# First row norm of a three-layer block: warm-up by products of zeros, rows turned by products with scaled identities, sinks written by ScalarE

## The chip, the cores and the metric

The kernel runs on one core of a Trainium2 chip. The metric is device time in microseconds (us), the median of several executions. A profiled execution gives the trace; its span runs from the first to the last instruction of the program, and the execution's own time lies a little above it.

## What is computed

The input x has 512 rows of 1024 channels, float32. A hybrid block (pooling branch and mLSTM branch) and two attention layers follow one another. Cut to what the change touches:

```python
def rms_norm(x, g):
    xf = x.astype(jnp.float32)
    y = xf * lax.rsqrt(jnp.mean(xf * xf, axis=-1, keepdims=True) + EPS)
    return (y * g.astype(jnp.float32)).astype(x.dtype)

h = rms_norm(x, norm_pre_g)              # [1, 512, 1024], the first norm
proj = jnp.einsum('bsd,de->bse', h, w_in)  # everything else of the block starts here
...
# even attention layer: 6 query heads with a window of 128 keys and one sink logit per head:
# the sink stands beside the keys in the softmax and has no value row
```

## The kernel before

**The stages.** The product of two float32 matrices is made of three products of reduced operands: each operand is split in a head (`hi`) and a rest (`lo`), both of the type float32r. ScalarE writes the heads of the weights and VectorE the rests (for a few units GpSimd writes both), and TensorE accumulates three products of 512 columns each (lines 1763 to 1765). The stages (gates, u, za, mix, ga, pa, qk, v, and so on up to the two attention layers) follow each other in an order that is written out by hand, one queue per engine; there is no planner. Weights come in units of 1 MB into three slots, loaded from SyncE's queue.

**The first norm.** The 512 rows are 4 tiles of 128 rows (`TT = 4`), the 1024 channels 8 tiles (`KT = 8`). TensorE needs the normalised rows with channels on the partitions, so each of the 32 blocks of 128x128 has to be turned. Four tiles of x are loaded on SyncE's queue, the identity on ScalarE's. ScalarE squares the tiles 0, 1 and 3 with a sum along each row (`square`, line 785) and takes the root (`root`, line 790); VectorE squares tile 2 itself (line 1234) and ScalarE takes its root at line 831. VectorE makes the reciprocal (line 1209) and scales the 1024 columns of the tile into `xnrow` (line 1210). TensorE first turns the identity 8 times for warm-up (`WARM`, line 1879), then turns the 8 blocks of each tile as it comes (line 1884), into eight banks, one per channel tile. Only the last row tile completes the banks and signals `tr_ready`. Then ScalarE writes the head of each of the 8 channel tiles with the gain (line 797), VectorE the rest (line 1216), and TensorE starts the first stage (gates), 24 products that each wait for their channel tile, and then the stage u, whose first weights VectorE splits behind the 8 rests (line 1185).

**The sinks.** In the even layer the probabilities of a pair of heads stand in `pr`, with the sink in the column behind the keys. For 12 pairs VectorE copies the sinks there (line 1652) just ahead of the two instructions that add the bias to the logits and find the least (line 1654). ScalarE takes the exponential over keys and sink (line 1134), and VectorE the reciprocal of its sum (line 1629). TensorE turns the probabilities (line 2162), VectorE copies them (line 1669), and TensorE multiplies them with the values (line 2174); between these TensorE computes the gate z of the same layer with products of the usual kind. GpSimd splits z's weights at the same time (lines 694 and 695).

Of the kernel before, what the change touches and what calls it, by code (L numbers as in the profile page):

```python
# [10 lines left out]
ACT = mybir.ActivationFunctionType  # L11
ALU = mybir.AluOpType
AX = mybir.AxisListType

P = 128
D = 1024
KT = D // P
S = 512
TT = S // P
# [1 line left out]
SLOT = KT * UC  # L21
SLOTS = 3
EPS = 1e-6
WARM = 8
BIG = 1e30
FLOOR = -3e38

# [19 lines left out]
A_HEADS, B_HEADS, C_HEADS, M_HEADS = 6, 6, 12, 4  # L47
# [7 lines left out]
VC = {}  # L55
# [65 lines left out]
def hybrid_block_then_two_attention_layers(nc, A, vecs_d, consts_d, out):  # L121
    stack = ExitStack()
    with stack:
        base = (nc.sbuf_base + 63) // 64 * 64
        K = 1024

        def at(name, shape, offset, dt=F32):
            return nc.alloc_sbuf_tensor_at(name, shape, dt, offset=base + offset)

        def sem(name):  # L130
            return stack.enter_context(nc.semaphore(name))


        HT, OP, RAW, WHI, R0, R1, R2, R3, R4, CST = (
            0, 32 * K, 64 * K, 88 * K, 112 * K, 128 * K, 144 * K, 160 * K, 177 * K, 193 * K)
# [11 lines left out]
        ident = at("ident", [P, P], CST)  # L147
        bones = at("bones", [P, P], CST + 512)
        vecs = at("vecs", [P, NVEC], CST + K)
# [12 lines left out]
        small = at("small", [P, 24], CST + 14 * K + 768)  # L162

        xrow = at("xrow", [P, TT, D], R4)
        xnrow = at("xnrow", [P, TT, D], R0)
        rowmax_all = at("rowmax_all", [P, 2, S], CST + 7 * K)
        zaT = at("zaT", [P, KT, S], R0)
        uT = at("uT", [P, KT, UW], R1)
# [36 lines left out]
        pr = at("pr", [P, 6, S], R0 + 4 * K)  # L205
# [20 lines left out]
        ident_in = sem("ident_in")  # L226
# [3 lines left out]
        x_in = [sem(f"x_in{t}") for t in range(TT)]  # L230
# [13 lines left out]
        eps_ready = sem("eps_ready")  # L244
        rsd_ready = sem("rsd_ready")
        xn_ready = sem("xn_ready")
        xsq_by_vector = sem("xsq_by_vector")
        tr_ready = sem("tr_ready")
        tr_hi = sem("tr_hi")
        tr_lo = sem("tr_lo")  # L250
# [45 lines left out]
        hn_done = sem("hn_done")  # L296
# [4 lines left out]
        prT_ready = sem("prT_ready")  # L301
# [3 lines left out]
        o_ready = sem("o_ready")  # L305
        x_rows = sem("x_rows")
        logit_ready = sem("logit_ready")
        part_hi_ready = sem("logit_operand_hi_by_scalar")
        part_split = sem("logit_operand_split_by_vector")
        stored = sem("stored")  # L310
# [96 lines left out]
        def first_bank(k):  # L407

            return acc[:, k, :] if k < 4 else aux[:, k - 4, :]
# [103 lines left out]
        def pr_slot(p, e):  # L513
            return 2 * (p % 3) + e
# [233 lines left out]
        def _(act):  # L748
            step = Steps(act, act_step)
# [3 lines left out]
            seen = {"rssq": 0, "rvar": 0, "tr": 0, "hi": 0, "hn": 0, "exp": 0, "unit": 0}  # L753
# [68 lines left out]
            act.wait_ge(act_first, 1)  # L822
            nc.scalar.activation(small[:, 13:14], small[:, 12:13], ACT.Sqrt)
            act.wait_ge(eps_ready, 1)
            for t in (0, 1, 3):
                act.wait_ge(x_in[t], 16)
                square(xrow, xnrow, t, 0)
                root(t)
                if t == 1:
                    act.wait_ge(xsq_by_vector, 1)  # L830
                    nc.scalar.activation(small[:, 2:3], small[:, 2:3], ACT.Sqrt, scale=1.0 / D,
                                         bias=small[:, 14:15]).then_inc(rsd_ready, 1)
            act.wait_ge(pre_gain_in, 16)
            heads_of_transposes("pre_g", ht_hi, S, first_bank)
            weight_heads(2)
# [106 lines left out]
            for h in range(HEADS):  # L942
# [12 lines left out]
                for t in range(TT):  # L955
# [5 lines left out]
                    if t:  # L961
# [3 lines left out]
                                         scale=small[:, 16 + 2 * (t % 2):17 + 2 * (t % 2)]).then_inc(hf_ready, 1)  # L965
# [52 lines left out]
            for t in range(TT):  # L1018
# [4 lines left out]
                                     bias=stats[:, 5, 2 * t:2 * t + 1]).then_inc(post_sd, 1)  # L1023
# [42 lines left out]
            for L, name in enumerate("eo"):  # L1066
# [52 lines left out]
                pairs = PAIRS[L]  # L1119
# [5 lines left out]
                    nc.scalar.activation(zT[:, hu % 2, :], z_bank, ACT.Tanh, scale=0.5).then_inc(th_ready, 1)  # L1125

                def probabilities_of(p):
                    for e, job in enumerate(pairs[p]):
                        i = 2 * p + e
                        act.wait_ge(nm_ready, 2 * pairs_done + i + 1)  # L1130
                        tile = pr[:, pr_slot(p, e), 0:job.keys + (job.sink is not None)]
                        if job.bias is None and pairs_done + p >= 3:
                            act.wait_ge(prT_ready, pairs_done + p - 2)
                        nc.scalar.activation(tile, tile if job.bias is not None else logit_bank(L, p, e)[:, 0:job.keys], ACT.Exp,  # L1134
                                             scale=-1.0, bias=stats[:, 1, i:i + 1],
                                             accum_out=stats[:, 2, i:i + 1]).then_inc(pr_ready, 1)
# [32 lines left out]
        def _(dve):  # L1169
            step = Steps(dve, dve_step)  # L1170
            seen = {"rssq": 0, "rsd": 0, "tr": 0, "t": 0, "lo": 0, "hn": 0, "arg": 0, "unit": 0}
            v = nc.vector
# [32 lines left out]
            def scale_rows(src, dst, t, col):  # L1205
                c = small[:, col + t:col + t + 1]
                seen["rsd"] += 1
                dve.wait_ge(rsd_ready, seen["rsd"])
                step(v.reciprocal(c, c))
                v.tensor_scalar(dst[:, t, :], src[:, t, :], c, None, ALU.mult).then_inc(xn_ready, 1)  # L1210
# [13 lines left out]
            def tile_written(ins):  # L1224
                ins.then_inc(t_ready, 1)
                seen["t"] += 1

            v.memset(small[:, 12:13], 1.0).then_inc(act_first, 1)
            v.memset(uT[:, :, 0:PAD], 0.0)
            v.memset(small[:, 14:15], EPS).then_inc(eps_ready, 1)  # L1230
            step(v.memset(uT[:, :, PAD + S:UW], 0.0))
            scale_rows(xrow, xnrow, 0, 0)
            dve.wait_ge(x_in[2], 16)
            v.tensor_tensor_reduce(out=xnrow[:, 2, :], in0=xrow[:, 2, :], in1=xrow[:, 2, :], scale=1.0, scalar=0.0,
                                   op0=ALU.mult, op1=ALU.add, accum_out=small[:, 2:3]).then_inc(xsq_by_vector, 1)
            for t in (1, 2, 3):
                scale_rows(xrow, xnrow, t, 0)
            dve.wait_ge(pre_gain_in, 16)
            rests_of_transposes("pre_g", ht_hi, ht_lo, S, first_bank)

# [5 lines left out]
            at_ = VC["b_if"]  # L1246
# [81 lines left out]
            for d in range(2):  # L1328
                ins = v.tensor_copy(gcol[:, :, d, :], gmT[:, :, 0, d, 0:HEADS])
# [5 lines left out]
            for u in range(units):  # L1335
                for half in range(2):
                    dve.wait_ge(acc_ready, u * 2 + 2 * a0 + 1 + half)
                    m = mergedT[:, 2 * u + half, :]
                    ins = v.tensor_tensor(m, acc[:, 2 * ((a0 + u) % 2) + half, :], m, ALU.mult)
# [10 lines left out]
            for u in range(units):  # L1350
                dve.wait_ge(acc_free, u + a0 + 1)
                for half in range(2):
# [6 lines left out]
                    for k in range(1, TAPS):  # L1359
                        ins = v.scalar_tensor_tensor(out_, cpad[:, slot, k:k + S], V("conv_w", j * TAPS + k), out_,  # L1360
                                                     ALU.mult, ALU.add)
# [50 lines left out]
            for c in range(2):  # L1412
# [3 lines left out]
                for t in range(TT):  # L1416
                    dve.wait_ge(v_hi_ready, TT * c + t + 1)
                    for e in range(2):
                        h = 2 * c + e
                        ins = v.tensor_tensor(v_lo[h][:, t, :], wide_bank(a0 + 2 * c, t)[:, HD * e:HD * e + HD],  # L1420
                                              v_hi[:, t, VW * h:VW * h + HD].bitcast(F32), ALU.subtract)
# [8 lines left out]
            for h in range(HEADS):  # L1430
                if 0 < h and h + 1 < HEADS:
                    rests_of_qk(h + 1)
                for t in range(TT):
                    i = TT * h + t
                    b = 2 * (t % 2)
                    c = 16 + 2 * (t % 2)
# [120 lines left out]
            for L, name in enumerate("eo"):  # L1557
# [65 lines left out]
                pairs = PAIRS[L]  # L1623
# [7 lines left out]
                def biased(p, e):  # L1631
                    job = pairs[p][e]
                    if done + p >= 3:
                        dve.wait_ge(prT_ready, done + p - 2)
                    dve.wait_ge(logit_ready, done + p + 1)
                    kind, h, slope = job.bias
                    least = stats[:, 1, 2 * p + e:2 * p + e + 1]
                    scale, start = 1.0, -FLOOR
                    if kind == "forget":
                        if job.t == 0:  # L1640
                            dve.wait_ge(csum_in[job.slot], 16 * (h // 3 + 1))
                        bias = csum_all[:, job.slot, 0:job.keys]
                    else:
                        full = masks2[:, 0:S] if kind == "dist" else masks2[:, S + P:S + P + 2 * WIN]
                        bias = full[:, full.shape[-1] - job.keys:]
                        scale = slope
                    if job.sink is not None:
                        start = V("sinks", job.sink)
                        if e == 0:

                            at_ = VC["sinks"] + job.sink
                            v.tensor_copy(pr[:, pr_slot(p, 0):pr_slot(p, 0) + 2, job.keys],
                                          vecs[:, at_:at_ + A_HEADS // 2 + 1:A_HEADS // 2])
                    v.tensor_tensor_reduce(out=pr[:, pr_slot(p, e), 0:job.keys], in0=logit_bank(L, p, e)[:, 0:job.keys],  # L1654
                                           in1=bias, scale=scale, scalar=start,
                                           op0=ALU.add, op1=ALU.min, accum_out=least).then_inc(nm_ready, 1)
# [100 lines left out]
        def _(pe):  # L1757
# [116 lines left out]
                    seen["tr"] += 1  # L1874


            pe.wait_ge(ident_in, 16)
            for n in range(WARM):
                nc.tensor.transpose(first_bank(0)[:, 0:P], ident[:], ident[:])
            for t in range(TT):  # L1880
                seen["xn"] += 1
                pe.wait_ge(xn_ready, seen["xn"])
                for k in range(KT):
                    ins = nc.tensor.transpose(first_bank(k)[:, P * t:P * t + P], xnrow[:, t, P * k:P * k + P], ident[:])
                    if t == TT - 1:
                        ins.then_inc(tr_ready, 1)
            seen["tr"] += KT
# [377 lines left out]
```

## Time and profile before

| | |
|---|---|
| median of 3 executions | 1150.04 us (1148.8 to 1150.35) |
| profiled execution, its own time | 1149.97 us |
| its span | 1148.2 us |
| TensorE busy | 1137.4 us, 99% |
| VectorE busy | 675.9 us, 59% |
| ScalarE busy | 594.6 us, 52% |
| GpSimd busy | 145.3 us, 13% |

The profile has, beside the page (shares by engine, slices of the span, the chain that ended last, the costliest groups), views of single stretches. PE is TensorE's product, PEld its weight load, DVE VectorE, ACT ScalarE, POOL GpSimd, SP SyncE. "128x512 f32" is partitions by elements; a number in the form 128*128 is the shape of the array that a product uses (contraction by output partitions). In names like `acc<-ident,xnrow` the operand that lies still in the array is the last one.

### The profile page before, as it was taken

What the parts mean: (1) busy time and instruction counts of PE and PEld (TensorE: products, weight loads), DVE (VectorE), ACT (ScalarE), POOL (GpSimd) and SP (SyncE); (2) the same over time, 40 slices, a digit from 0 to 9 for tenths busy, and PEclk for the clock granted to TensorE, in tenths of its full rate; (3) what the DMA queues carried; (4) which work ended last, traced back from release to release, by engine and by line L of the source; (5) the groups of instructions that cost most, each with busy time, mean ns of one, the idle gap of its engine ahead of it and who ended that gap; (6) DMA issues with size and microseconds to landing.
All of it is one profiled execution on the core that took longest, in us unless ns stands there. A gap on an engine that the chain in (4) does not pass through costs nothing.

```text
span 1148.2 us, 15655 instructions
## 1 busy us (share of the span) xinstructions
PE 1137.4 (99%) x6158; PEld 944.7 (82%) x6158; DVE 675.9 (59%) x1187; ACT 594.6 (52%) x1038; POOL 145.3 (13%) x153
## 2 busy tenths in 40 slices
PE   7999999999999999999999999999999999999998
PEld 6888888888888888888889888777888888887887
DVE  5484523488755676524547677777445674766631
ACT  5533431244436766733337577777433687577720
POOL 1000000000000000000000004443223000723531
PEclk9999999999999999999999999999999999999999
DMA  6323223233231221332445233212223323122221
GB/s 192 125 80 110 86 99 115 75 109 110 92 110 56 92 92 38 127 110 74 150 141 131 74 107 77 74 38 75 74 74 112 109 75 117 59 79 83 71 74 74
DMA packets 108081, 107.91 MB, mean 94 GB/s; under 512 B 18076, under 2 KB 93212, under 8 KB 108008
## 3 DMA queue, kind: packets, MB, share of 16 engines
q1 hardware_dynamic: 106504, 101.67, 28.7%
q10 hardware_dynamic: 1504, 5.24, 1.2%
q8 instruction: 49, 0.80, 0.3%
q14 instruction: 24, 0.20, 0.1%
HBM read 104.64 MB, written 2.25 MB: 93 GB/s over the span
## 4 chain that ended last, share of the span: by engine, by line
PE 97%; ACT 1%; DVE 1%; DMA 0%; issue 0%; DVEq 0%; ACTq 0%
PE acc L1763 24%; PE acc L1765 24%; PE acc L1764 24%; PE aux L2174 3%; PE aux L1763 3%; PE aux L2162 3%; PE aux L1765 3%; PE aux L1764 3%; PE acc L2128 3%; PE aux L1955 1%; PE aux L1957 1%; PE aux L1956 1%; PE aux L1855 1%; PE aux L2006 1%; PE aux L2005 1%; ACT pr L1134 0%
## 5 line engine op out<-in xcount | busy, mean ns | idle before, releaser
L1763 PE MATMUL acc<-ht_hi,whi 128*128 128x512 f32 x728 | 284.3, 391 | 1.0 <-DVE ht_lo L1216 1.0
L1765 PE MATMUL acc<-ht_hi,wlo 128*128 128x512 f32 x728 | 283.4, 389 | 0.0
L1764 PE MATMUL acc<-ht_lo,whi 128*128 128x512 f32 x728 | 283.3, 389 | 0.0
L1192 DVE TENSOR_TENSOR wlo<-raw,whi 128x2048 fp32r<-128x2048 f32 x68 | 155.6, 2288 | 106.4 <-ACT whi L770 99.7
L694 POOL TENSOR_SCALAR whi<-raw 128x512 fp32r<-128x512 f32 x68 | 49.1, 722 | 942.8 <-DMA raw<-e_w_in_dram 708.0
L1763 PEld LDWEIGHTS acc<-ht_hi,whi 128*128 128x128 f32 x728 | 136.7, 188 | 29.8 <-issue 1.2
L1765 PEld LDWEIGHTS acc<-ht_hi,wlo 128*128 128x128 f32 x728 | 136.6, 188 | 28.4
L1764 PEld LDWEIGHTS acc<-ht_lo,whi 128*128 128x128 f32 x728 | 136.7, 188 | 27.9
L770 ACT ACTIVATE whi<-raw 128x2048 fp32r<-128x2048 f32 x68 | 129.9, 1910 | 51.1 <-DMA raw<-w_in_dram 22.5
L695 POOL TENSOR_TENSOR wlo<-raw,whi 128x512 fp32r<-128x512 f32 x68 | 91.8, 1350 | 5.7
L1763 PE MATMUL acc<-whi,ht_hi 128*128 128x512 f32 (+1 forms) x224 | 83.9, 375 | 0.0
L1765 PE MATMUL acc<-whi,ht_lo 128*128 128x512 f32 (+1 forms) x224 | 83.8, 374 | 0.0
L1764 PE MATMUL acc<-wlo,ht_hi 128*128 128x512 f32 (+1 forms) x224 | 83.7, 374 | 0.0
L1141 ACT ACTIVATE pr<-pr,stats 128x256 f32<-128x256 f32 (+3 forms) x128 | 61.0, 525 | 20.8 <-DVE stats L1629 20.4
L1669 DVE COPY prT<-aux 128x256 f32<-128x256 f32 (+3 forms) x128 | 52.1, 448 | 27.5 <-PE aux L2162 27.3
L1765 PE MATMUL acc<-op_hi,wlo 128*128 128x512 f32 x144 | 56.0, 389 | 0.0
L1763 PE MATMUL acc<-op_hi,whi 128*128 128x512 f32 x144 | 56.0, 389 | 0.0
L1764 PE MATMUL acc<-op_lo,whi 128*128 128x512 f32 x144 | 56.0, 389 | 0.0
L1763 PE MATMUL aux<-ht_hi,whi 128*128 128x512 f32 x128 | 55.7, 435 | 0.0
L1134 ACT ACTIVATE pr<-pr,stats 128x257 f32<-128x257 f32 (+5 forms) x96 | 51.1, 533 | 8.1 <-DVE stats L1654 8.1
L1763 PE MATMUL acc<-whi,op_hi 128*128 128x512 f32 x128 | 50.6, 396 | 0.0
L1765 PE MATMUL aux<-ht_hi,wlo 128*128 128x512 f32 x128 | 50.6, 395 | 0.0
(274 smaller groups left out, 2016.5 us busy)
## 6 DMA issues: line engine op xcount, KB each, us to landing
raw<-w_in_dram SPq DMA_DIRECT2D x72, 512.0 KB, 4.6
raw<-o_w_in_dram SPq DMA_DIRECT2D x28, 512.0 KB, 4.7
raw<-e_w_in_dram SPq DMA_DIRECT2D x14, 512.0 KB, 5.1
raw<-w_proj_pool_dram SPq DMA_DIRECT2D x8, 512.0 KB, 4.0
raw<-w_proj_mlstm_dram SPq DMA_DIRECT2D x8, 512.0 KB, 4.1
raw<-w_out_dram SPq DMA_DIRECT2D x8, 512.0 KB, 4.6
raw<-o_w_out_dram SPq DMA_DIRECT2D x8, 512.0 KB, 4.7
raw<-e_w_in_dram SPq DMA_DIRECT2D x14, 256.0 KB, 3.9
```

The lines of the kernel that those rows point to most:

```text
L694: step(nc.gpsimd.tensor_scalar(whi[:, slot, piece], raw[:, slot, piece], 1.0, 1.0, ALU.mult, ALU.mult))
L695: ins = nc.gpsimd.tensor_tensor(wlo[:, slot, piece], raw[:, slot, piece], whi[:, slot, piece].bitcast(F32), ALU.subtract)
L770: nc.scalar.activation(whi[:, slot, :], raw[:, slot, :], ACT.Copy).then_inc(w_hi, 1)
L1134: nc.scalar.activation(tile, tile if job.bias is not None else logit_bank(L, p, e)[:, 0:job.keys], ACT.Exp, scale=-1.0, bias=stats[:, 1, i ...
L1141: nc.scalar.activation(tile, tile, ACT.Copy, scale=stats[:, 4, 2 * p + e:2 * p + e + 1]).then_inc(norm_ready, 1)
L1192: v.tensor_tensor(wlo[:, slot, :], raw[:, slot, :], whi[:, slot, :].bitcast(F32), ALU.subtract).then_inc(w_split, 1)
L1669: ins = v.tensor_copy(prT[L][2 * (k % 2) + e][:, 0:job.keys], trans_bank(e)[:, 0:job.keys])
L1763: mm(out_, w_hi_, x_hi, start=first, stop=False)
L1764: mm(out_, w_hi_, x_lo, start=False, stop=False)
L1765: return mm(out_, w_lo_, x_hi, start=False, stop=last)
L2128: ins = mm(logit_bank(L, p, e)[:, lo:hi], q[qp:qp + HD2, rows], k[kp:kp + HD2, keys][:, lo:hi], start=n == 0 and not forget, stop=n == 2)
L2162: ins = nc.tensor.transpose(trans_bank(e)[:, P * b:P * b + P], pr[:, pr_slot(k, e), P * b:P * b + P], ident[:])
```

## The change

The warm-up no longer waits for the identity: VectorE zeroes a tile of 128x128 with its first instruction, and TensorE multiplies it with itself 32 times instead of turning the identity 8 times. ScalarE squares and roots all four row tiles in order. VectorE no longer scales the rows; it waits for the identity and writes, for each row tile, the identity with each row times that row's reciprocal root (128x128 instead of 128x1024 elements). TensorE multiplies each 128x128 block of x itself with that scaled identity, a plain product in float32 where before it was a transpose of the normalised block. The later norms are left as they are. In the even layer ScalarE writes the sinks of a pair, ahead of its wait for the logits, and the exponential of the pair's first head waits for that copy.

```diff
-WARM = 8
+WARM = 32
...
+        factors = at("factors", [P, TT, P], OP)
+        zeros = at("zeros", [P, P], OP + 2 * K)
...
-            for t in (0, 1, 3):
+            for t in range(TT):
                 act.wait_ge(x_in[t], 16)
                 square(xrow, xnrow, t, 0)
                 root(t)
-                if t == 1:
-                    act.wait_ge(xsq_by_vector, 1)
-                    nc.scalar.activation(small[:, 2:3], small[:, 2:3], ACT.Sqrt, scale=1.0 / D,
-                                         bias=small[:, 14:15]).then_inc(rsd_ready, 1)
...
                 def probabilities_of(p):
+                    if pairs[p][0].sink is not None:
+                        if p >= 3:
+                            act.wait_ge(prT_ready, p - 2)
+                        elif p == 0:
+                            act.wait_ge(hn_done, seen["hn"])
+                        at_ = VC["sinks"] + pairs[p][0].sink
+                        nc.scalar.activation(pr[:, pr_slot(p, 0):pr_slot(p, 0) + 2, pairs[p][0].keys],
+                                             vecs[:, at_:at_ + A_HEADS // 2 + 1:A_HEADS // 2], ACT.Copy).then_inc(sink_ready, 1)
                     for e, job in enumerate(pairs[p]):
                         i = 2 * p + e
                         act.wait_ge(nm_ready, 2 * pairs_done + i + 1)
+                        if e == 0 and job.sink is not None:
+                            act.wait_ge(sink_ready, p + 1)
...
+            v.memset(zeros[:], 0.0).then_inc(zeros_ready, 1)
             v.memset(small[:, 12:13], 1.0).then_inc(act_first, 1)
...
-            scale_rows(xrow, xnrow, 0, 0)
-            dve.wait_ge(x_in[2], 16)
-            v.tensor_tensor_reduce(out=xnrow[:, 2, :], in0=xrow[:, 2, :], in1=xrow[:, 2, :], scale=1.0, scalar=0.0,
-                                   op0=ALU.mult, op1=ALU.add, accum_out=small[:, 2:3]).then_inc(xsq_by_vector, 1)
-            for t in (1, 2, 3):
-                scale_rows(xrow, xnrow, t, 0)
+            dve.wait_ge(ident_in, 16)
+            for t in range(TT):
+                c = small[:, t:t + 1]
+                seen["rsd"] += 1
+                dve.wait_ge(rsd_ready, seen["rsd"])
+                step(v.reciprocal(c, c))
+                v.tensor_scalar(factors[:, t, :], ident[:], c, None, ALU.mult).then_inc(factors_ready, 1)
...
-                        if e == 0:
-
-                            at_ = VC["sinks"] + job.sink
-                            v.tensor_copy(pr[:, pr_slot(p, 0):pr_slot(p, 0) + 2, job.keys],
-                                          vecs[:, at_:at_ + A_HEADS // 2 + 1:A_HEADS // 2])
...
-            pe.wait_ge(ident_in, 16)
+            pe.wait_ge(zeros_ready, 1)
             for n in range(WARM):
-                nc.tensor.transpose(first_bank(0)[:, 0:P], ident[:], ident[:])
+                mm(first_bank(0)[:, 0:P], zeros[:], zeros[:], start=True, stop=True)
             for t in range(TT):
-                seen["xn"] += 1
-                pe.wait_ge(xn_ready, seen["xn"])
+                pe.wait_ge(factors_ready, t + 1)
                 for k in range(KT):
-                    ins = nc.tensor.transpose(first_bank(k)[:, P * t:P * t + P], xnrow[:, t, P * k:P * k + P], ident[:])
+                    ins = mm(first_bank(k)[:, P * t:P * t + P], xrow[:, t, P * k:P * k + P], factors[:, t, :],
+                             start=True, stop=True)
                     if t == TT - 1:
                         ins.then_inc(tr_ready, 1)
```

## Rows read from the trace of the kernel before

**Rows 1.** The page: busy us (share) xinstructions; TensorE's granted clock; chain by engine.

```profile
PE 1137.4 (99%) x6158; PEld 944.7 (82%) x6158; DVE 675.9 (59%) x1187; ACT 594.6 (52%) x1038; POOL 145.3 (13%) x153
...
PEclk9999999999999999999999999999999999999999
...
PE 97%; ACT 1%; DVE 1%; DMA 0%; issue 0%; DVEq 0%; ACTq 0%
```

**Rows 2.** TensorE's waits, whole span: us in total, times, longest.

```profile
PE acc L1884 <- DVE xnrow L1210: 0.5, 1, 0.5
PE aux L2162 <- DVE prT L1669: 0.5, 1, 0.5
```

**Rows 3.** The chain that ended last, first 30 us: start us, us, what.

```profile
7.21 1.20 DVE xnrow L1234
...
9.34 1.11 PE acc L1884 x4
...
13.17 0.70 ACT ht_hi L797
```

**Rows 4.** Timeline of the opening: start us, us, what, xcount, [idle before <-releaser].

```profile
0.85 0.11 DVE L1229 MEMSET uT<- 128x64 f32 x1
...
4.67 1.06 ACT L785 ACTIVATE xnrow<-xrow 128x1024 f32<-128x1024 f32 x1 [2.00 <-DMA xrow<-x_dram]
...
4.83 1.97 PE L1879 MATMUL acc<-ident 128*128 128x128 f32 x8 [4.83 <-DMA ident<-consts_dram]
...
5.85 0.29 ACT L790 ACTIVATE small<-small 128x1 f32<-128x1 f32 x1
6.05 1.04 ACT L785 ACTIVATE xnrow<-xrow 128x1024 f32<-128x1024 f32 x1
...
9.34 1.11 PE L1884 MATMUL acc<-ident,xnrow 128*128 128x128 f32 x4
...
10.25 1.06 PE L1884 MATMUL aux<-ident,xnrow 128*128 128x128 f32 x4
...
10.39 0.75 DVE L1210 TENSOR_SCALAR xnrow<-xrow,small 128x1024 f32<-128x1024 f32 x1
...
12.80 0.60 PE L1884 MATMUL acc<-ident,xnrow 128*128 128x128 f32 x4
...
13.17 2.43 ACT L797 ACTIVATE ht_hi<-acc,vecs 128x512 fp32r<-128x512 f32 x4 [3.00 <-PE acc L1884]
13.23 0.60 PE L1884 MATMUL aux<-ident,xnrow 128*128 128x128 f32 x4
...
20.52 0.19 PEld L1763 LDWEIGHTS acc<-ht_hi,whi 128*128 128x128 f32 x1 [0.37 <-DVE wlo L1185]
```

**Rows 5.** Line 1884: duration ns min/median/max, first and last start.

```profile
L1884 PE MATMUL acc<-ident,xnrow x16: 272/421/475, 7.3 to 13.1; 128*128 128x128 f32 x16
```

**Rows 6.** Lines 2174 and 2162, in the same columns.

```profile
L2174 PE MATMUL aux<-prT,mv x128: 272/273/324, 802.0 to 1109.1; 128*64 128x128 f32 x128
...
L2162 PE MATMUL aux<-ident,pr x286: 270/273/332, 725.0 to 1105.4; 128*128 128x128 f32 x143
```

**Rows 7.** Timeline, one group of line 2174 near the end.

```profile
1108.33 1.09 PE L2174 MATMUL aux<-prT,mv 128*64 128x128 f32 x16
```

**Rows 8.** Line 1652 (the sinks), and the page's group of line 1134.

```profile
L1652 DVE COPY pr<-vecs x12: 146/363/1266, 720.4 to 749.0; 128x2 f32<-128x2 f32 x12
...
L1134 ACT ACTIVATE pr<-pr,stats 128x257 f32<-128x257 f32 (+5 forms) x96 | 51.1, 533 | 8.1 <-DVE stats L1654 8.1
```

**Rows 9.** Timeline around the longest copy of sinks.

```profile
730.30 1.29 POOL L695 TENSOR_TENSOR wlo<-raw,whi 128x512 fp32r<-128x512 f32 x1
730.35 1.27 DVE L1652 COPY pr<-vecs 128x2 f32<-128x2 f32 x1
...
731.91 0.40 ACT L1134 ACTIVATE pr<-pr,stats 128x129 f32<-128x129 f32 x1 [1.40 <-DVE stats L1654]
...
732.87 0.33 PE L2162 MATMUL aux<-ident,pr 128*128 128x128 f32 x1 [0.53 <-DVE prT L1669]
```

More of the change, by code:

```diff
@@ L246, in hybrid_block_then_two_attention_layers @@
         xn_ready = sem("xn_ready")
-        xsq_by_vector = sem("xsq_by_vector")
+        zeros_ready = sem("zeros_ready")
+        factors_ready = sem("factors_of_rows_ready")
         tr_ready = sem("tr_ready")
@@ L307, in hybrid_block_then_two_attention_layers @@
         logit_ready = sem("logit_ready")
+        sink_ready = sem("sink_ready")
         part_hi_ready = sem("logit_operand_hi_by_scalar")
```

## The prediction

> **What bounds the kernel now.** I read the page first. TensorE is busy for 99% of the span and holds 97% of the chain that ended last [rows 1], so the time moves only by what moves TensorE's stream or fills one of its waits. Its own waits, read next, are short [rows 2]: 0.5 us in the first norm for `xnrow`, 0.5 us once in the even attention for a copy of turned probabilities. The chain at the start [rows 3] shows how the opening ends: VectorE's work on tile 2, then from 9.34 on only TensorE turning blocks, then ScalarE's first head at 13.17. So tile 1 was awaited there, but tiles 2 and 3 (the last scaling ends at 10.39 + 0.75 = 11.14 [rows 4]) stood ready while TensorE was still working through the backlog. The opening is bound by TensorE's own speed.
>
> That speed has two levels. A transpose of 128x128 takes 421 ns in the median and 272 at the least [rows 5]. Starts tell the price better, as neighbours overlap [rows 4]: 12 transposes start between 10.25 and 12.80, which is 0.213 us each; the next four take 13.23 - 12.80, 0.108 us each. The ratio of two is that of the clock's two levels, 1.2 and 2.4 GHz; the page's clock line reads 9 throughout [rows 1] and does not show this rise, so the durations decide. The rise came at about 12.8. Before it TensorE had turned identities from 4.83 on, with pauses, and blocks without a pause from 9.34 on [rows 4].
>
> **The first signal is what the sum is made on.** The eight heads, the eight rests and the 24 products of the first stage follow the first finished bank at ScalarE's pace (2.43 us for four heads, 0.61 each [rows 4]). Neither 0.108 nor 0.22 us per block is slower than 0.61, so all that follows keeps its shape and shifts with the first bank: its last block started at 12.80 and ended at 12.80 + 0.27 = 13.07. Behind it I find no slack that would swallow a shift: VectorE's rests run into the split of the next weights, TensorE waits 0.37 us for it at 20.52 [rows 4], and from there it is busy almost without a gap [rows 1]. These waits are for engines that start late by as much. A shift D of the first bank is a shift of the end.
>
> **Warm-up and turning, edit by edit.** Removed: the wait for the identity (4.83), 8 identity transposes, 32 transposes, one square on VectorE, four scalings of 0.75 us. Added: 32 products of zeros, four scalings of 128 columns, one square on ScalarE, 32 plain products.
>
> *Producers.* The squares on ScalarE start 6.05 - 4.67 = 1.38 us apart [rows 4]: 4.67, 6.05, 7.43, 8.81. Each root ends 1.47 us behind its square's start (5.85 + 0.29 - 4.67). A reciprocal and the scaling of 128 columns, an eighth of the 0.75, add about 0.45. The factors are then ready at 6.6, 8.0, 9.3 and 10.7, the last 0.4 us earlier than `xnrow`'s last tile. This would be the gain, were TensorE free.
>
> *Price of a plain float32 product.* The nearest rows are the products of probabilities and values, line 2174 [rows 6, 7]. The program makes 32 of them with `mv` in each of two layers (8 pairs, 2 heads, 2 blocks), 64 in all, and the trace has 128 records: two records, each with its weight load, for one product. Line 2162, transposes, has 286 records, and the blocks of keys that the code turns there are 134 in the even layer and 152 in the odd one: one record each. The 16 records of one group take 1.09 us [rows 7]; they are 8 products, two heads side by side in two halves of the array, so 8 steps in 1.09 - 0.27, about 0.11 us a step once the longer first one is set aside. A product that fills the array has no partner: two steps, 0.218 us at the fast level, and at half the clock 0.427. Read at face value, without "side by side", the same group gives 1.09/8, 0.11 to 0.14 us per product; that is the lower bound. The upper bound is a load of full width that is not hidden, twice as much as I take (0.436 and 0.85). I take 0.218 and 0.427, twice the transpose.
>
> The Trainium skill, page "TensorE: Matmul & The Clock Gate", section "Terms", says that transpose mode is four times faster for float32. In these rows I find two, from 0.108 to 0.218 us. By the page's factor put on this kernel's transposes the sum would be that of the upper bound; it is a rival below.
>
> *The warm-up overruns.* Zeros are ready at about 0.95 (VectorE's neighbouring fills take 0.11 us [rows 4]). All 32 products at the slow level would last 13.7 us, at the fast one 7.0. Let r be the moment of the rise. The warm-up ends at W = r + (32 - (r - 0.95)/0.427) x 0.218 = 0.49 r + 7.46. From the rows, r lies between 0.95 + (12.8 - 9.34) = 4.4, as after the unbroken stretch, and 0.95 + (12.8 - 4.83) = 8.9, as after the first identity. Products without a pause are like the stretch, though more work lay before that; I take 6.2, and W = 10.5. By then the factors of three tiles wait, and the fourth are ready long before their turn. The first bank ends after 24 blocks of 0.218 and its own 0.38 (the second record starts 0.11 later and lasts 0.27): W + 5.61 = 16.1. D = 16.1 - 13.07 = 3.0 us later, in general 0.49 r. It would be 2.2 with r = 4.4, and 4.4 with r = 8.9. ScalarE's fourth square hides under this backlog. What is late next is TensorE itself; a shorter warm-up would have shown the producers. If the fill of zeros is held up by GpSimd's fills of 0.95 us at the start, D grows by 0.5 us.
>
> **Sinks.** Twelve copies leave VectorE; the median is 363 ns, the least 146, the longest 1266 [rows 8]. The longest runs beside a GpSimd instruction that began 0.05 us earlier and ends 0.03 before it; behind it ScalarE stood idle for 1.40 us and TensorE for 0.53 [rows 9]. This wait of TensorE is the one of 0.5 in its list [rows 2], and I count it as gained, with 0.1 for delays under TensorE's overlap: -0.6 us. The other eleven copies end in no listed wait of TensorE. On ScalarE a copy of two columns costs like its other tiny instructions, up to 0.29 us [rows 4]. Queued behind it are the two exponentials and what follows. The added wait for `prT_ready` is one that the logits' instruction on VectorE has already, so it holds nothing up that was not held. ScalarE sits idle ahead of line 1134 for 8.1 us in all, for VectorE [rows 8], and I cost the copies at nothing. Without that cover they would cost 12 x 0.29 = 3.5 us; at the other end nothing more than 0.8 us comes back.
>
> The Trainium skill, page "SBUF — State Buffer", section "SBUF: two separate sides", says that some VectorE copies and GpSimd lock each other out of a shared pair of ports and that ScalarE never waits on anyone. The rows of the 1266 ns copy agree. What ScalarE's copy costs beside GpSimd no row here shows.
>
> **Sum.** +3.0 - 0.6 = +2.4 us. On the profiled execution (1149.97, that is its span of 1148.2 and 1.8 around it) this gives 1152.4; the median of the runs shown is 0.07 above that execution, so I predict 1152.5.
>
> **Rivals.**
>
> *A plain product costs no more than a transpose* (faster). Place: the 64 products at the start. At face value rows 7 give 0.11 per product. Then by 6.2 the warm-up has done 24.6 products and ends at 7.0; TensorE waits for factors, and the first bank ends at 10.7 + 0.27 + 0.1 = 11.1, 2.0 before 13.07; with the sinks -2.6, 1147.4. With price p the first bank ends at about 3.8 + 57 p, so this side begins at p = 0.16 us. Against it: the two records per product [rows 6]. Chance 0.08.
>
> *The level is high almost at once* (r about 1 to 2). D is 0.5 to 1.0, with the sinks near nothing: 1150.2. For it: nothing shows the level before 4.83. Against: it was low at 4.83 and for 8 us of work. Chance 0.07.
>
> *Zeros don't lift the clock.* All 32 run slowly, W = 14.6, and the level rises only 3.5 us into the real products: 8 of those slow, 16 fast (3.5 us), first bank at 14.6 + 3.5 + 3.5 + 0.4 = 22.0; D = 8.9, 1158.3. For it: these operands switch nothing. Against: the identity is nearly all zeros, too. Chance 0.05.
>
> *A product costs four transposes*, 0.436 and 0.85. W = 6.2 + 25.8 x 0.436 = 17.5, first bank at 17.5 + 24 x 0.436 + 0.7 = 28.6, D = 15.6: 1165. Against it: rows 7, unless a half-width load is what hides there. Chance 0.04.
>
> *ScalarE's copies of sinks bind* in the even attention: +3.5 instead of nothing, 1156.0. Against: its idle time there. Chance 0.04.
>
> **How the numbers follow.** The forecast (warm-up overruns, r between 4.4 and 8.9, net +1.5 to +3.8) has 0.72. About what a measurement can tell from no change is 0.2%, 2.3 us. Within the forecast this bound is crossed for r above 5.9, which I hold for 0.62 of its cases. Slower: 0.72 x 0.62 + 0.13 = 0.58. Same: 0.27 + 0.07, rounded up to 0.35. Faster: 0.07, the rest of the first rival. The range goes from 1150.6 (just above the early rise) to 1155.0 (the latest rise, with the fill held up and some cost on ScalarE); what lies outside is about 0.2.
>
> **What would show it.** The warm-up has 64 records from about 1 us on, 0.213 us apart and then 0.11, and ends near 10.5. The line of the turning products has 64 records, the first bank's last one ends near 16; no wait of TensorE stands between them; ScalarE's first head starts near 16.2 and the stage u's first product near 23.5, all 3 us later. TensorE's wait of 0.5 us for `prT` is gone, and the sinks on ScalarE take 0.2 to 0.3 us each within its idle time. Wrong: one record per product, a wait of TensorE for the factors, or a first head before 13.2.

## The result and the profile after

The changed kernel takes 1152.49 us in the median of 16 runs (1151.59 to 1153.14), the kernel before 1149.69 in 16 runs beside it (1148.3 to 1150.72). The ratio is 1.0025, 95% interval 1.0018 to 1.0031: slower by 0.25%, about 2.8 us. The profiled execution took 1152.93 us with a span of 1150.9, 2.7 above the span of before.

The page of the changed kernel: TensorE is still the bound, and its 88 additional records (6246 against 6158) are 128 - 40, which is 64 products in two records each less 40 transposes in one.

```profile
PE 1145.5 (100%) x6246; PEld 954.0 (83%) x6246; DVE 668.1 (58%) x1174; ACT 597.2 (52%) x1052; POOL 144.0 (13%) x153
```

The opening, from its timeline (columns as in [rows 4]); line 1886 are the zeros, 1890 the turning products:

```profile
0.83 0.17 DVE L1238 MEMSET zeros<- 128x128 f32 x1 [0.83 <-PEq L2262]
...
1.05 9.49 PE L1886 MATMUL acc<-zeros 128*128 128x128 f32 x64 [1.05 <-DVE zeros L1238]
...
10.38 1.06 PE L1890 MATMUL acc<-factors,xrow 128*128 128x128 f32 x8
...
10.64 0.39 DVE L1249 TENSOR_SCALAR factors<-ident,small 128x128 f32<-128x128 f32 x1
...
15.74 1.06 PE L1890 MATMUL acc<-factors,xrow 128*128 128x128 f32 x8
16.23 2.42 ACT L801 ACTIVATE ht_hi<-acc,vecs 128x512 fp32r<-128x512 f32 x4 [5.82 <-PE acc L1890]
...
16.63 1.06 PE L1890 MATMUL aux<-factors,xrow 128*128 128x128 f32 x8
...
23.57 0.19 PEld L1770 LDWEIGHTS acc<-ht_hi,whi 128*128 128x128 f32 x1 [0.38 <-DVE wlo L1195]
```

Between 10.38 and 16.63 stand 56 records, 0.1116 us each, so a product (two records) takes 0.223 us. The moment at which the clock rose follows from the zeros' 64 records. The last of them starts at 1.05 + 9.49 - 0.275 = 10.27. The first step is 0.16 us longer than its neighbours; without this excess the 63 steps share 9.06 us. A step is 0.2133 us at half the clock and 0.1117 at the full one, so 19.9 were at half, and the clock rose at 1.05 + 0.16 + 19.9 x 0.2133, about 5.5. ScalarE's first head starts at 16.23 where it started at 13.17 [rows 3], 3.06 later, and TensorE's wait for the first weights of u stands at 23.57 instead of 20.52 [rows 4], 3.05 later, with the same length. All four tiles' factors were there by 11.03; TensorE never waited for them.

TensorE's waits in the changed kernel:

```profile
PE acc L1886 <- DVE zeros L1238: 1.1, 1, 1.1
PE aux L1962 <- DVE hrow L1456: 0.4, 1, 0.4
PE acc L1770 <- DVE orow L1517: 0.3, 1, 0.3
```

The wait for `prT` of [rows 2] is gone, and one of 0.3 us for `orow` is new. I matched the 6118 records of products behind the opening one to one in both traces. Their distance jumps at two places only and otherwise drifts by about 0.1 us at most. It is 3.06 at the first, near 3.0 for most of the way, and 3.03 at 588 us. At the first product of `w_out`'s second half, behind the transposes of the memory rows, it becomes 3.46, and 3.52 some 60 us on. Just ahead of the second jump it is 3.47. In the even attention, at the very transpose that had waited [rows 9], it falls to 2.78, and one product on to 2.72, where it stays to the end. The rows for the first jump, first of before, then of after; the last row of after lies behind the second jump, whose row of before is in [rows 9]:

```profile
583.26 1.92 ACT L770 ACTIVATE whi<-raw 128x2048 fp32r<-128x2048 f32 x1 [9.65 <-DMA raw<-w_out_dram]
...
588.91 0.47 PE L1763 MATMUL acc<-whi,ht_hi 128*128 128x512 f32 x1
```

```profile
586.73 1.92 ACT L774 ACTIVATE whi<-raw 128x2048 fp32r<-128x2048 f32 x1 [10.11 <-DMA raw<-w_out_dram]
...
588.68 2.29 DVE L1202 TENSOR_TENSOR wlo<-raw,whi 128x2048 fp32r<-128x2048 f32 x1 [4.35 <-ACT whi L774]
...
590.89 0.68 DVE L1517 TENSOR_TENSOR orow<-acc,gpost 128x512 f32<-128x512 f32 x1
...
592.37 0.47 PE L1770 MATMUL acc<-whi,ht_hi 128*128 128x512 f32 x1 [0.27 <-DVE orow L1517]
...
735.65 0.60 PE L2169 MATMUL aux<-ident,pr 128*128 128x128 f32 x4
```

A load of `w_out` landed 0.4 us later than the shift: ScalarE's split of it, which waits for the load in both traces, began at 583.26 before and at 586.73 now. VectorE's share of the split came late by as much, and behind it the scaling of the row on which TensorE waits. The ledger: +3.06 - 0.03 + 0.43 + 0.06 - 0.05 - 0.75 = +2.72 us.

The sinks on ScalarE, durations in ns (min/median/max), which answer to the first row of [rows 8]:

```profile
L1134 ACT ACTIVATE pr<-vecs x12: 188/190/197, 723.9 to 752.7; 128x2 f32<-128x2 f32 x12
```

### The profile page after: what moved, and what is told of

The parts are those of the page before. It is cut to its first block, busy times and chain, and to the rows that moved or that the text cites. A ratio compares the mean times of both kernels' runs of the same rounds, so it can differ in the third digit from the quotient of the medians.

```text
span 1150.9 us, 15844 instructions
## 1 busy us (share of the span) xinstructions
PE 1145.5 (100%) x6246; PEld 954.0 (83%) x6246; DVE 668.1 (58%) x1174; ACT 597.2 (52%) x1052; POOL 144.0 (13%) x153
## 4 chain that ended last, share of the span: by engine, by line
PE 98%; ACT 1%; DVE 1%; DMA 1%; issue 0%; SPq 0%; DVEq 0%; ACTq 0%
PE acc L1770 24%; PE acc L1772 24%; PE acc L1771 24%; PE aux L1770 3%; PE aux L1772 3%; PE aux L1771 3%; PE aux L2181 3%; PE aux L2169 3%; PE acc L2135 3%; PE acc L1886 1%; PE aux L1962 1%; PE aux L1964 1%; PE aux L1963 1%; PE aux L1862 1%; PE aux L2013 1%; PE aux L2012 1%
```

## The experiments

Ratios are against the kernel before, run on the same chip in the same job. "Shift" is the distance of matched products from those of before, in the profiled executions.

**1. The sinks alone.** The kernel before with those parts of the diff that move the sinks:

```diff
-                            v.tensor_copy(pr[:, pr_slot(p, 0):pr_slot(p, 0) + 2, job.keys],
...
+                        nc.scalar.activation(pr[:, pr_slot(p, 0):pr_slot(p, 0) + 2, pairs[p][0].keys],
...
```

> The kernel before with only the sinks moved to ScalarE. Theory (the copy of 1266 ns beside GpSimd delayed the chain into TensorE once, ScalarE has idle time for its own copies): the opening is that of before (first head near 13.2 us), TensorE's wait of 0.5 us for prT is gone, the span is 0.6 to 0.8 us shorter, ratio about 0.9994. Rival (ScalarE's copies bind in the even attention): 12 x 0.2 to 0.29 us more, +2 to +3.5 us less the gain. Rival (the 0.5 us wait only moves to the next engine): no change.

Measured: 1148.78 us, ratio 0.9991 (0.9982 to 1.0000). The shift falls from -0.46 to -1.15 at the transpose of [rows 9] and to -1.21 one product on, 0.75 us in all. TensorE's longest waits in this run; that for `prT` is not among them:

```profile
PE acc L1885 <- DMA ident<-consts_dram: 5.0, 1, 5.0
PE acc L1769 <- DVE ht_lo L1227: 1.0, 1, 1.0
PE acc L1890 <- DVE xnrow L1221: 0.5, 1, 0.5
PE aux L1961 <- DVE hrow L1455: 0.4, 1, 0.4
```

The theory holds; neither rival shows. The trace shows it better than the median does, as the interval of the ratio reaches 1. The opening, which is not changed, was 0.57 us shorter by itself:

```profile
4.98 1.97 PE L1885 MATMUL acc<-ident 128*128 128x128 f32 x8 [4.98 <-DMA ident<-consts_dram]
...
11.24 0.71 PE L1890 MATMUL acc<-ident,xnrow 128*128 128x128 f32 x4
11.79 0.60 PE L1890 MATMUL aux<-ident,xnrow 128*128 128x128 f32 x4
12.23 0.60 PE L1890 MATMUL acc<-ident,xnrow 128*128 128x128 f32 x4
```

Groups of four transposes are already 0.44 us apart from about 11.5 on, not from 12.8: the clock's rise is not at the same moment in each execution.

**2. The norm alone.** The changed kernel with the sinks written by VectorE as before.

> The changed kernel with the sinks left on VectorE, so the first norm's part alone. Theory (warm-up and products overrun, all else follows): first head near 16.2 us, 3.05 us later than before, and the end 3.0 to 3.6 us later, since the wait for prT is back; ratio about 1.0028. Rival (part of the 2.7 us measured came from the moved sinks): the shift at the end is under 2.5 us. The weights of w_out landed 0.5 us late in the changed kernel's profile; if that belongs to the shift it comes again here, if it is chance it need not.

Measured: 1153.78 us, ratio 1.0033 (1.0020 to 1.0045).

```profile
1.05 9.96 PE L1881 MATMUL acc<-zeros 128*128 128x128 f32 x64 [1.05 <-DVE zeros L1228]
...
16.69 2.42 ACT L801 ACTIVATE ht_hi<-acc,vecs 128x512 fp32r<-128x512 f32 x4 [6.52 <-PE acc L1885]
```

```profile
PE aux L2164 <- DVE prT L1671: 0.5, 1, 0.5
```

The shift is 3.52 at the first head, 0.5 more than expected: the same sum as above puts the rise at 6.4, one us later than in the changed kernel. It is still near 3.5 in the even attention up to the last sinks, with the 0.5 us wait back, and 3.97 at the end. The step of 0.42 stands at the products with the values at 756.77, where TensorE waits 0.20 us for a copy of turned probabilities:

```profile
754.30 1.75 DVE L1222 TENSOR_TENSOR op_lo<-zT,op_hi 128x512 fp32r<-128x512 f32 x1
755.97 0.74 DVE L1671 COPY prT<-aux 128x256 f32<-128x256 f32 x2
```

The instruction ahead of this copy took 1.18 us at the same place before (at 749.86) and 1.75 here. Run 8 below, the other run with a shifted opening and sinks on VectorE, has the same step; no run with sinks on ScalarE has it. One execution of each can't tell whether it belongs to the sinks or to how the engines' work happens to meet. So the first norm is what costs, and the sinks gave part of it back. No step stands at `w_out`, so the late load of the changed kernel is not bound to the shift.

**3. Half the warm-up.** `WARM = 16` in the changed kernel.

> The changed kernel with 16 products of zeros instead of 32. Theory (the warm-up's length is what costs): zeros begin at 1.05, the clock rises near 5.5 as it did, so 10.4 products run slowly and the rest at 0.2234 us: the warm-up ends near 6.8, before the first factors at 6.95; TensorE then waits for factors, the fourth at 11.03, and the first bank ends near 11.4, 1.6 us before the kernel before's 13.07. With the sinks -2.2 us against before, about 1147.5, and 5 us under the changed kernel. Rival (the price of the products alone makes the loss, 32 x 0.2234 = 7.1 us against the transposes): the first bank would end near 6.95 + 7.1 = 14.1 or later, +0.4 us against before. Rival (TensorE's pauses between tiles let the clock fall again): products at 0.427 us, first bank at 13 or later.

Measured: 1149.12 us, ratio 0.9994 (0.9986 to 1.0003).

```profile
1.05 5.32 PE L1886 MATMUL acc<-zeros 128*128 128x128 f32 x32 [1.05 <-DVE zeros L1238]
...
6.99 1.16 PE L1890 MATMUL acc<-factors,xrow 128*128 128x128 f32 x8 [0.63 <-DVE factors L1249]
7.99 1.06 PE L1890 MATMUL aux<-factors,xrow 128*128 128x128 f32 x8
...
8.88 1.06 PE L1890 MATMUL acc<-factors,xrow 128*128 128x128 f32 x8
...
12.94 2.42 ACT L801 ACTIVATE ht_hi<-acc,vecs 128x512 fp32r<-128x512 f32 x4 [2.52 <-PE acc L1890]
```

The loss is gone, 3.4 us of it against the changed kernel, but my theory for the amount was wrong. The rival on the price was right in what binds, though not in its number: it asked for 14.1 or later at the first bank and a loss of 0.4, as it counted all 32 products where 24 and the bank's own stand ahead. I had TensorE wait for the factors of each tile. It waited once, 0.6 us for the first, and never again: 8 products take 8 x 0.223 = 1.79 us, longer than the 1.38 between two tiles. The first head came at 12.94 instead of 11.5. The products bound the opening even without the overrun. This run had the step at `w_out`, too (0.7 us, from -0.31 to 0.40), against it.

**4. The warm-up kept, the blocks turned by transposes.** VectorE scales the rows again:

```diff
+                seen["xn"] += 1
+                pe.wait_ge(xn_ready, seen["xn"])
...
-                    ins = mm(first_bank(k)[:, P * t:P * t + P], xrow[:, t, P * k:P * k + P], factors[:, t, :],
-                             start=True, stop=True)
+                    ins = nc.tensor.transpose(first_bank(k)[:, P * t:P * t + P], xnrow[:, t, P * k:P * k + P], ident[:])
```

> The changed kernel, 32 products of zeros, but VectorE scales the rows and TensorE turns them by transposes as before. It parts the 3.06 us at the first bank into warm-up and price. Theory: the warm-up ends at 10.3, 24 transposes at 0.109 take 2.6, the first bank ends at 13.2, +0.1 us against before, so 2.8 us of the 3.06 are the dearer products behind an overlong warm-up; with the sinks about -0.5 us against before (1149.2). Rival (a plain product is no dearer than a transpose in effect): as the changed kernel, 1152.5.

Measured: 1149.77 us, ratio 0.9999 (0.9990 to 1.0008).

```profile
1.05 9.71 PE L1881 MATMUL acc<-zeros 128*128 128x128 f32 x64 [1.05 <-DVE zeros L1238]
...
10.60 0.60 PE L1887 MATMUL acc<-ident,xnrow 128*128 128x128 f32 x4
...
13.22 0.60 PE L1887 MATMUL acc<-ident,xnrow 128*128 128x128 f32 x4
13.59 2.42 ACT L801 ACTIVATE ht_hi<-acc,vecs 128x512 fp32r<-128x512 f32 x4 [3.27 <-PE acc L1887]
```

The 24 transposes between 10.60 and 13.22 take 0.109 us each, half a product. The first head comes 0.42 us after that of before; 0.22 of it is the warm-up, which ended at 10.60 instead of 10.38 (the clock rose at 5.9). Without that, 0.20 is left of the 3.06, and 2.9 us are the price of the products, as the theory has it. Against the kernel before it takes both to lose: the overrun alone costs 0.2 to 0.4, and the products without it (run 3) still end with the first bank 0.2 us before the old one.

**5. Half the warm-up and transposes.** Run 4 with `WARM = 16`.

> 16 products of zeros, VectorE scales the rows, TensorE turns them by transposes; sinks on ScalarE. Theory (a plain product costs 0.2234 us and a transpose 0.109, and 32 x 0.2234 is more than the tiles' own time, 32 x 0.109 is not): the warm-up ends near 6.4, TensorE turns each tile in 0.9 us and waits for the next, 1.38 us apart; the last tile is scaled at 11.3, the first bank ends near 11.7, 1.4 us before the kernel before's 13.07, with the sinks -2.0 us, about 1147.8. Rival (pauses of half a microsecond let the clock fall): transposes at 0.213 us, first bank at 12.5 or later, no more than -1.2 us in all.

Measured: 1148.14 us, ratio 0.9986 (0.9977 to 0.9995).

```profile
7.64 0.63 PE L1887 MATMUL acc<-ident,xnrow 128*128 128x128 f32 x4 [0.40 <-DVE xnrow L1220]
...
10.77 0.79 DVE L1220 TENSOR_SCALAR xnrow<-xrow,small 128x1024 f32<-128x1024 f32 x1
11.62 0.66 PE L1887 MATMUL acc<-ident,xnrow 128*128 128x128 f32 x4 [0.31 <-DVE xnrow L1220]
12.04 2.42 ACT L801 ACTIVATE ht_hi<-acc,vecs 128x512 fp32r<-128x512 f32 x4 [1.50 <-PE acc L1887]
```

Now TensorE waits for the producers, and pauses of up to half a microsecond left the clock up (groups of four still take 0.60 to 0.66). The theory holds, 0.3 us later than expected, since x's first tile came later (4.96 instead of 4.67). The four runs side by side, first head in us (13.17 before):

| | turned by products | turned by transposes |
|---|---|---|
| 32 products of zeros | 16.23 | 13.59 |
| 16 products of zeros | 12.94 | 12.04 |

The overrun costs 3.29 us with products and 1.55 with transposes; the products cost 2.64 us behind the overrun and 0.90 without it. Some tenths of each are the moment of the clock's rise and x's arrival in these executions.

**6. Mixed.** Run 5, with the last row tile turned by products (TensorE's part, against run 5; VectorE writes the last tile's factors instead of scaling it):

```diff
-                    ins = nc.tensor.transpose(first_bank(k)[:, P * t:P * t + P], xnrow[:, t, P * k:P * k + P], ident[:])
+                    if t == TT - 1:
+                        ins = mm(first_bank(k)[:, P * t:P * t + P], xrow[:, t, P * k:P * k + P], factors[:, t, :],
+                                 start=True, stop=True)
+                    else:
+                        ins = nc.tensor.transpose(first_bank(k)[:, P * t:P * t + P], xnrow[:, t, P * k:P * k + P], ident[:])
```

> As the run above, but the last row tile is turned by products with the scaled identity, the other three by transposes. Theory: the last factors are ready at 10.95, 0.4 us before the last scaled tile; the first bank's two records end 0.38 us later, at 11.35, and the banks then follow 0.2234 apart, still under ScalarE's 0.61 per head: -1.7 us at the first bank, with the sinks -2.4 us, about 1147.5. Rival (the product's price wins even there): no better than the run above.

Measured: 1147.73 us, ratio 0.9984 (0.9975 to 0.9993), the best of all, 4.8 us under the changed kernel. In the profiled runs its first head comes 0.56 us before run 5's, of which 0.24 are the earlier x; the medians are 0.4 apart. The ratios' intervals overlap, as they carry the spread of the kernel before; of the runs themselves, nine of these eleven (1147.5 to 1148.11) lie under the fastest of run 5 (1147.94 to 1148.61). The theory holds.

```profile
10.53 0.32 DVE L1251 TENSOR_SCALAR factors<-ident,small 128x128 f32<-128x128 f32 x1
...
10.90 1.16 PE L1898 MATMUL acc<-factors,xrow 128*128 128x128 f32 x8
11.48 2.42 ACT L801 ACTIVATE ht_hi<-acc,vecs 128x512 fp32r<-128x512 f32 x4 [1.19 <-PE acc L1898]
```

**7. A quarter of the warm-up.** `WARM = 8` in the changed kernel.

> The changed kernel with 8 products of zeros. They end near 4.5 and TensorE idles until the first factors at 6.95. If the work before the pause does not carry the clock over it, the products start at 0.427 us each and the clock rises some 3.4 to 4.5 us into them: first bank near 14.6, +1.5 us against before, with the sinks +0.9. Rival (the clock is up by then, near 5.5 as with 32): as with 16, first bank near 12.85.

Measured: 1150.63 us, ratio 1.0007 (0.9998 to 1.0016).

```profile
1.05 3.65 PE L1886 MATMUL acc<-zeros 128*128 128x128 f32 x16 [1.05 <-DVE zeros L1238]
...
6.96 1.30 PE L1890 MATMUL acc<-factors,xrow 128*128 128x128 f32 x8 [2.26 <-DVE factors L1249]
...
8.04 1.92 PE L1890 MATMUL aux<-factors,xrow 128*128 128x128 f32 x8
...
11.37 1.06 PE L1890 MATMUL aux<-factors,xrow 128*128 128x128 f32 x8
...
14.53 2.42 ACT L801 ACTIVATE ht_hi<-acc,vecs 128x512 fp32r<-128x512 f32 x4 [4.16 <-PE acc L1890]
```

The sum came out as expected, by another course. The 16 records end at 4.7; the last of them is short already (0.275 us), so the clock had risen at 4.4. TensorE then idles 2.26 us. The first eight records (four products) behind the pause start at the fast rate for the most part, the next two groups take 1.92 and 1.78 us instead of 1.06, and from about 11.2 on they are fast again. The trace's granted clock says the same: full from 6.96 to 7.8, half from 7.9 to 11.2, full from 11.3 on. The pause itself cost nothing in the first products behind it and was paid for by the later ones.

**8. Transposes as warm-up.** `WARM = 48` identities in the kernel before.

> The kernel before with 48 identity transposes instead of 8, to see when transposes alone, unbroken from about 4.9, raise the clock: with the zeros it took 4.4 us. If transposes count like products, the start distance goes from 0.213 to 0.109 us 3.4 to 5 us after their start, at 8.3 to 9.9, and the 48 end near 12.3. If they count less, all 48 run at 0.213 and end near 15.1.

Measured, one execution: 1151.82 us.

```profile
4.82 7.13 PE L1879 MATMUL acc<-ident 128*128 128x128 f32 x48 [4.82 <-DMA ident<-consts_dram]
```

48 transposes at half the clock would take 10.2 us. In 7.13 fit 16 of 0.213 us and 31 of 0.109, so the clock rose at about 8.3, 3.5 us after the start. Transposes without a pause raised it here, too, within the time that the zeros took (3.1 to 5.4 us after their start). The kernel before and run 1, with pauses between their transposes, took 8.0 and 6.5 us from the first identity. So the pauses, not the kind of the work, are the likely cause of the late rise at 12.8; that is argued, since a run with zeros and the same pauses was not made, and two such executions are few for a moment that varies.

## Why the prediction was right

The forecast was 1152.5; 1152.49 was measured. That it is so close is luck. The forecast change was +2.4 us and the measured one is +2.8, and the level that the sum started from, 1150.04, lay 0.35 above the median of the kernel before in the runs beside it. Within the change, too, terms off by some tenths cancel: without the late load of `w_out` the profiled execution would have been 2.3 later, not 2.7.

- *TensorE alone bounds the opening, and a shift of the first bank is a shift of the end.* Right: 3.06 at the first head, 3.05 at the stage u, 3.03 at 588 us.
- *A plain product is two records of 0.109, twice a transpose.* Right, with 64 records on each line. The size was 0.223 instead of 0.218. Reading the pairs of line 2174 as running side by side was the step on which the sign hung: at face value (0.11) the forecast would have been a gain. Run 4 tests it: transposes in the place of the products bring 2.64 us of the 3.06 back. By the factor of four of the Trainium skill ("TensorE: Matmul & The Clock Gate", section "Terms"), it would have been a loss of 15 us; runs 3 and 4 show two.
- *The warm-up overruns to W = 10.5.* It ended at 10.38, where the turning products begin. The rise was taken at 6.2 and came at 5.5 (-0.34 us in W), the zeros began at 1.05 instead of 0.95, and the dearer product gave the rest back. Over all runs that start with zeros the rise lay between 4.2 and 6.4, within the stated bounds of 4.4 and 8.9 but for one, and in their lower half.
- *"A shorter warm-up would have shown the producers."* Wrong, as run 3 shows. The step that failed is the comparison that I didn't make: eight products, 1.79 us, against 1.38 between tiles. It did not touch the sum, since TensorE was late anyway.
- *Producers.* The last factors came at 11.03, not at 10.7; the scaling of 128 columns takes 0.29 us, not an eighth of 0.75, and x's first tile came 0.16 later than before. Off the path.
- *Sinks, -0.6 us.* It was -0.75 here and in each of the six other runs with the sinks on ScalarE, at the place that was named. On ScalarE the copy takes 190 ns beside GpSimd's work (at 723.94 and 735.93, for example) as elsewhere, at most 197. That agrees with the Trainium skill ("SBUF — State Buffer", section "SBUF: two separate sides"), by which ScalarE never waits on anyone.
- *Not foreseen:* +0.43 us from the late load of `w_out`. The step is also in run 3 (0.7), is about 0.2 or less in runs 1 and 4 to 8, of either sign, and missing in 2; it goes with neither part of the change. Why the load is late was not tried.

## What to carry to other kernels

Compare the work that an edit puts on the bound engine with the interval at which its input comes: a transpose of 0.109 us kept pace with tiles 1.38 us apart, a product of 0.223 did not, though it spared another engine most of its work. Make a warm-up end when the first input is ready, no later; here 16 products of zeros did it, 32 ended 3.4 us behind the first factors, and with 8 the gap was paid for behind it. Use the dearer form only where its shorter chain ends last, as for the last tile in run 6.

## What was not expected of the hardware

- The moment at which the clock rises varies by 2.2 us between executions that start the same products of zeros at 1.05 (4.2, 4.4, 5.5, 5.5, 5.9, 6.0 and 6.4). Where the warm-up overruns, each microsecond is worth about half of one: run 2 rose 1.0 later than the changed kernel and its first head came 0.46 later. In the kernel before it was 12.8 in one execution and 11.5 in another (run 1), and the opening was 0.57 us shorter.
- After a pause of 2.3 us the first four products ran fast and only then the others slowly, for over 3 us (run 7): a pause can cost where no wait stands.
